# Convolution released ahead of the affine part, early transposes, residual products and a later last affine in a two-layer transformer kernel

## What is computed

```python
def short_conv_mixer(h, w_in, conv_w, conv_b, w_out):
    gb, gc, u = jnp.split(h @ w_in, 3, axis=-1)
    up = jnp.pad(gc * u, ((0, 0), (1, 1), (0, 0)))
    y = up[:, :-2] * conv_w[0] + up[:, 1:-1] * conv_w[1] + up[:, 2:] * conv_w[2] + conv_b
    return (gb * y) @ w_out

for l in range(DEPTH):
    ...
    u_lat = modulate(h_lat, m[0], m[1])
    ...
    h_lat = post_norm(h_lat, m[2] * y_lat, ln_w[l, 0], ln_b[l, 0])
    tokens = modulate(h_lat, m[3], m[4]).reshape(B * S, D)
    ...
    y = hier_moe(tokens, router_wg[l], router_bg[l], router_we[l], router_be[l], moe_w1[l], moe_w3[l], moe_w2[l])
    h_lat = post_norm(h_lat, m[5] * y[:B * S].reshape(B, S, D), ln_w[l, 1], ln_b[l, 1])
    ...
```

## Time and profile before

| | |
|---|---|
| median of three runs | 2521.5 us |
| the profiled execution: time, span | 2521.79 us, 2520.0 us |
| TensorE busy | 2326.1 us, 92% |
| VectorE, ScalarE, GpSimd busy | 30%, 17%, 11% |
| mean granted clock of TensorE | 0.962 |
| share of TensorE in the chain that ended last | 75% |
| share of DMA, VectorE in that chain | 10%, 7% |

### The profile page before, as it was taken

One profiled execution on the slowest core, in us unless ns is written; L12 is line 12 of the kernel. 1 busy time (PEld: TensorE's weight loads), 2 busy tenths in 40 slices (PEclk: granted clock), 3 DMA queues, 4 the chain that ended last, 5 costly groups with the idle time before them and its releaser, 6 DMA issues.

```text
span 2520.0 us, 28374 instructions
## 1 busy us (share of the span) xinstructions
PE 2326.1 (92%) x10444; PEld 1168.0 (46%) x10444; DVE 768.3 (30%) x1753; ACT 419.2 (17%) x912; POOL 280.7 (11%) x341
## 2 busy tenths in 40 slices
PE   6999999999995999999898699999995999999987
PEld 3556547887553344344343244444553343443332
DVE  2683115555545111111113411111344111111115
ACT  2301224443121101011013100000111101101111
POOL 0000104232223000000000000000232000000000
PEclk9999999999996999999999799999996999999998
DMA  9881000001127999999967010101009999999956
GB/s 386 303 330 45 1 0 2 2 18 55 58 75 305 420 421 412 417 395 421 421 278 263 19 50 25 50 25 67 25 34 378 420 421 409 413 406 421 421 222 250
DMA packets 137069, 572.28 MB, mean 227 GB/s; under 512 B 25033, under 2 KB 50793, under 8 KB 84458
## 3 DMA queue, kind: packets, MB, share of 16 engines
q1 hardware_dynamic: 123690, 536.97, 53.5%
q0 software_dynamic: 13248, 33.57, 3.4%
HBM read 549.51 MB, written 35.65 MB: 232 GB/s over the span
## 4 chain that ended last, share of the span: by engine, by line
PE 75%; DMA 10%; DVE 7%; SPq 2%; issue 2%; ACT 1%; POOL 1%; DVEq 0%; POOLq 0%; ACTq 0%
PE bank L1038 20%; PE bank L1110 13%; PE bank L1060 10%; PE bank L658 8%; DMA bigA<-in_moe_w 7%; PE bank L965 4%; PE bank L925 4%; PE bank L761 3%; PE bank L615 3%; DVE lnwb L1451 2%; SPq L428 2%; PE bank L775 1%; PE bank L1126 1%; PE bank L744 1%; POOL bigC L2026 1%
## 5 line engine op out<-in xcount | busy, mean ns | idle before, releaser
L1038 PE MATMUL bank<-bigA,bigB 128*32 128x512 f32 (+2 forms) x1968 | 472.4, 606 | 16.4 <-DMA bigA<-in_moe_w 11.9
L1110 PE MATMUL bank<-bigB,bigA 128*128 128x512 f32 x768 | 332.8, 596 | 20.8 <-DVEq L1949 20.8
L658 PE MATMUL bank<-bigC,bigB 128*128 128x512 f32 (+3 forms) x768 | 295.0, 540 | 0.0
L1060 PE MATMUL bank<-bigA,bigB 128*32 128x512 f32 (+2 forms) x1120 | 272.7, 607 | 14.7 <-DMA bigA<-in_moe_w 12.2
L1038 PEld LDWEIGHTS bank<-bigA,bigB 128*32 128x32 f32 (+2 forms) x1968 | 163.1, 137 | 258.1 <-issue 252.7
L1038 PE MATMUL bank<-bigC,bigB 128*128 128x512 f32 (+2 forms) x720 | 265.7, 599 | 9.2 <-DMA bigA<-in_moe_w 6.0
L1110 PEld LDWEIGHTS bank<-bigB,bigA 128*128 128x128 f32 x768 | 146.9, 191 | 206.3 <-issue 206.3
L658 PEld LDWEIGHTS bank<-bigC,bigB 128*128 128x128 f32 x768 | 144.3, 195 | 128.4 <-issue 119.5
L1171 ACT ACTIVATE bigB<-bank,small 128x128 f32<-128x128 f32 x288 | 107.6, 460 | 421.4 <-PE bank L615 421.4
L1060 PEld LDWEIGHTS bank<-bigA,bigB 128*32 128x32 f32 (+2 forms) x1120 | 98.9, 140 | 161.0 <-issue 156.7
L1038 PEld LDWEIGHTS bank<-bigC,bigB 128*128 128x128 f32 (+2 forms) x720 | 91.1, 151 | 134.0 <-issue 129.9
(11 more groups left out here) (278 smaller groups left out, 2298.9 us busy)
## 6 DMA issues: line engine op xcount, KB each, us to landing
bigA<-in_moe_w SPq DMA_DIRECT2D x292, 1024.0 KB, 21.5
bigC<-in_moe_w SPq DMA_DIRECT2D x92, 1024.0 KB, 23.2
bigA<-in_ada_w SPq DMA_DIRECT2D x40, 1024.0 KB, 7.2
bigA<-y_rows SPq DMA_DIRECT2D x16, 1024.0 KB, 4.9
bigA<-in_w_in_odd SPq DMA_DIRECT2D x24, 512.0 KB, 6.0
bigA<-in_ada_w SPq DMA_DIRECT2D x4, 2048.0 KB, 12.5
bigC<-in_w_in_even SPq DMA_DIRECT2D x4, 2048.0 KB, 14.3
h_rows<-bigC SPq DMA_DIRECT2D x16, 512.0 KB, 2.6
```

What stands on the lines that cost most here:

```text
L658: last = mm(bank(n % 3)[:, 0:w], uT[:, k, t * P:(t + 1) * P], wring[:, g % 2, k, at_:at_ + w], start=(k == 0), stop=(k == KC - 1))
L1038: last = mm(bank(m)[at_:at_ + w, :], xT[:, j, KC // 2 * h + k, at_:at_ + w], w13_at[SLOT_OF[m, h, q][0]][:, k, :], start=(h == 0 and k == ...
L1060: last = mm(bank(6 + n)[at_:at_ + w, :], gT[:, 2 * h + k, at_:at_ + w], w2_at[SLOT_OF[2, h, q][0]][:, k, n * 512:(n + 1) * 512], start=(h ...
L1110: last = mm(bank(3 * half + m), wc[:, j, m, k, :], u1T[:, k, half * 512:(half + 1) * 512], start=(k == 0), stop=(k == KC - 1))
```

## The change

- TensorE transposes the rows of steps 0 and 1 of the experts before it starts on step 0; step 1's go to banks 6 and 7 and are counted on `u_ev` and `u_ev_d`. Later steps keep their place. GpSimd's program is not changed; its gather for step 3 waits for the transposes of step 1, so it is released with them.
- Of tiles 0 and 1 at a layer's end, the products of alpha and the rows (`residual_part`) are issued right after the experts and wait for `hback` on a semaphore of its own; `combined` adds the experts' rows when `pair` is there. The sums use banks 4, 5 and 0, 1.
- In layer 0 the gate rows follow `combined(0, 0)` and `combined(0, 1)` on TensorE and ScalarE, in place of both ahead of them; banks of `stream_T` are changed to fit.
- VectorE clears the edges and raises `conv_d` before the eight affines of layer 0, not after them.
- In layer 1 the affine of tile t - 1 follows the statistics of tile t.

```diff
@@ -555,7 +555,7 @@
...
                 for t in range(2):
-                    load(hback[:, t], h_dram[l][t * P:(t + 1) * P, :], f"pair_in{t}")
+                    load(hback[:, t], h_dram[l][t * P:(t + 1) * P, :], f"x_in{t}")
                 with sp.Fori(0, OVER // 2) as i:
...
@@ -1017,16 +1017,20 @@
...
 
-                def gathered_T(b, j, loads):
+                def gathered_T(b, j, loads, at_=2):
 
                     pe.wait_ge(S(f"xg_in{l}_{j}"), 16 * loads)
-                    transposes(xg[:, j], 2).then_inc(S(f"x_T{l}"), 1)
+                    transposes(xg[:, j], at_).then_inc(S(f"x_T{l}"), 1)
 
...
                     if m == 0:
-                        pe.wait_ge(S(f"xT_ev{l}"), 2 * (b + 1))
+                        if b == 1:
+                            pe.wait_ge(S("u_ev"), 2 * NTC - 2 + l + 1)
+                            pe.wait_ge(S("u_ev_d"), 2 + l + 1)
+                        else:
+                            pe.wait_ge(S(f"xT_ev{l}"), max(2 * b, 2))
                         if b:
...
@@ -1062,14 +1066,16 @@
...
 
+
                 gathered_T(0, 0, 1)
+                gathered_T(1, 1, 1, 6)
                 for b in range(NB):
...
                     hidden_half(b, 1)
-                    gathered_T(b + 1, (b + 1) % 2, (b + 1) // 2 + 1)
                     if b:
+                        gathered_T(b + 1, (b + 1) % 2, (b + 1) // 2 + 1)
                         output(b - 1)
...
@@ -1077,7 +1083,7 @@
...
                     b = 2 * i + j
-                    pe.wait_ge(S(f"xT_ev{l}"), 2 * (b + 1))
+                    pe.wait_ge(S(f"xT_ev{l}"), 2 * b)
                     pe.wait_ge(S(f"silu_a{l}"), b)
...
@@ -1111,37 +1117,53 @@
...
 
+
+            def sum_at(t):
+                return (4, 0)[t % 2]
+
+            def residual_part(l, t):
+
+                if t < 2:
+                    pe.wait_ge(S(f"x_in{t}"), (128, 112)[t] + 16 * (l + 1))
+                else:
+                    pe.wait_ge(S(f"pair_in{t % 2}"), 112 * l + 16 + 32 * (t // 2))
+                    pe.wait_ge(S("nrm"), NT * (2 * l + 1) + t - 1)
+                for n in range(2):
+                    mm(bank(sum_at(t) + n), alpha_i[:, :], hback[:, t % 2, n * 512:(n + 1) * 512], start=True, stop=False,
+                       skip_group_check=True)
+
             def combined(l, t):
...
                     pe.wait_ge(S("share_ok"), l + 1)
-                pe.wait_ge(S(f"pair_in{t % 2}"), 32 * (NT // 2 * l + t // 2 + 1))
-                if t >= 2:
-                    pe.wait_ge(S("nrm"), NT * (2 * l + 1) + t - 1)
+                if t < 2:
+                    pe.wait_ge(S(f"pair_in{t}"), 112 * l + 16)
+                else:
+                    residual_part(l, t)
                 for n in range(2):
-                    cols_n = slice(n * 512, (n + 1) * 512)
-                    dst = bank(4 + 2 * (t % 2) + n)
-                    mm(dst, alpha_i[:, :], hback[:, t % 2, cols_n], start=True, stop=False)
                     for k in range(2):
-                        last = mm(dst, share[:, k, t, :], pair[:, t % 2, k, cols_n], start=False, stop=(k == 1))
+                        last = mm(bank(sum_at(t) + n), share[:, k, t, :], pair[:, t % 2, k, n * 512:(n + 1) * 512],
+                                  start=False, stop=(k == 1), skip_group_check=True)
                 last.then_inc(S("comb"), 1)
...
                 n = NT + t
-                if t == 0:
-                    pe.wait_ge(S("gate_ev"), 4)
-                if t >= 2:
+                if t < 2:
+                    pe.wait_ge(S("gate_ev"), t + 3)
+                else:
                     pe.wait_ge(S("tile_a"), n - 1)
                     pe.wait_ge(S("tile_d"), n - 1)
-                transposes(hh[:, t], 2 * (t % 2)).then_inc(S("tile_T"), 1)
+                transposes(hh[:, t], (2, 6)[t % 2]).then_inc(S("tile_T"), 1)
 
             moe(0)
-            gate_rows(2, diag1[:, 0], 0)
-            gate_rows(3, diag1[:, 1], 2)
+            for t in range(2):
+                residual_part(0, t)
             for t in range(NT):
                 combined(0, t)
+                if t < 2:
+                    gate_rows(t + 2, diag1[:, t], (2, 6)[t])
                 if t:
...
@@ -1155,6 +1177,8 @@
...
             moe(1)
+            for t in range(2):
+                residual_part(1, t)
             for t in range(NT):
...
@@ -1303,9 +1327,9 @@
...
 
-                def rows_T(b, j):
+                def rows_T(b, j, at_=2, done=f"xT_ev{l}"):
                     act.wait_ge(S(f"x_T{l}"), b + 1)
-                    modulated(xT[:, j], 2, mod_of(l, 1), f"xT_ev{l}")
+                    modulated(xT[:, j], at_, mod_of(l, 1), done)
 
...
@@ -1316,13 +1340,14 @@
...
                 rows_T(0, 0)
+                rows_T(1, 1, 6, "u_ev")
                 for b in range(NB):
...
                         gated(b - 1)
-                    rows_T(b + 1, (b + 1) % 2)
+                        rows_T(b + 1, (b + 1) % 2)
                 gated(NB - 1)
...
@@ -1358,17 +1383,17 @@
...
 
-                ln(2 * l + 1, t, banks[2 + t % 2][:, :])
+                ln(2 * l + 1, t, banks[(2, 0)[t % 2]][:, :])
 
...
                 act.wait_ge(S("tile_T"), NT + t + 1)
-                modulated(u1T[:, :, t * P:(t + 1) * P], 2 * (t % 2), normed_mod(1), "tile_a")
-
-            gate_row(2, 0, 0)
-            gate_row(3, 1, 2)
+                modulated(u1T[:, :, t * P:(t + 1) * P], (2, 6)[t % 2], normed_mod(1), "tile_a")
+
             for t in range(NT):
                 combined(0, t)
+                if t < 2:
+                    gate_row(t + 2, t, (2, 6)[t])
                 if t:
...
@@ -1869,12 +1894,13 @@
...
                 rows_T(0, 0)
+                rows_T(1, 1, 6, "u_ev_d")
                 for b in range(NB):
...
                     gate_up(b)
-                    rows_T(b + 1, (b + 1) % 2)
                     if b:
+                        rows_T(b + 1, (b + 1) % 2)
                         scattered(b - 1)
...
@@ -1899,7 +1925,7 @@
...
                 for n in range(2):
-                    half_stats(banks[2 + t % 2], n)
+                    half_stats(banks[(2, 0)[t % 2]], n)
                 ln_stats(2 * l + 1, t)
...
@@ -1932,15 +1958,13 @@
...
                 dve.wait_ge(S("tile_T"), NT + t + 1)
-                modulated(u1T[:, :, t * P:(t + 1) * P], 2 * (t % 2), normed_mod(1), "tile_d")
+                modulated(u1T[:, :, t * P:(t + 1) * P], (2, 6)[t % 2], normed_mod(1), "tile_d")
 
...
             stream_T(NT - 1)
-            for t in range(NT):
-                affine(0, t)
             dve.wait_ge(S("wa2_in"), 208)
...
@@ -1948,6 +1972,8 @@
...
             v.sem_inc(S("z_ok"), 2)
+            for t in range(NT):
+                affine(0, t)
             with dve.Fori(0, KC // 2) as i:
...
@@ -1979,7 +2005,9 @@
...
                 combined(1, t)
-                affine(1, t)
+                if t:
+                    affine(1, t - 1)
+            affine(1, NT - 1)
 
...
```

## The result

| | before | after |
|---|---|---|
| median (lowest to highest), four executions each | 2521.94 us (2520.18 to 2522.47) | 2497.56 us (2496.97 to 2498.24) |
| span of the profiled execution | 2520.0 us | 2495.2 us |
| mean granted clock of TensorE | 0.962 | 0.967 |
| TensorE, VectorE, ScalarE, GpSimd busy | 92%, 30%, 17%, 11% | 93%, 31%, 17%, 11% |

After over before is 0.9905, with a 95% interval of 0.9887 to 0.9922. The change takes off 24.4 us; the forecast was 2497.3 us. Of the executions on this page one, of `release_alone`, was slow (2554.08 us at a mean granted clock of 0.922) and is in no comparison.

A forecast was written before the change was run, and what follows sets the result against it. TensorE carries 75% of the chain, but full DMA engines set the expert stages' end. 19.1 + 1.8 + 2.8 + 0.5 + 0 = 24.2 us off 2521.8, less 0.3 to the median, gives 2497.3 us; range 2493.0 to 2500.8 with the near rivals.

The forecast's parts named there:

- A, the release: Layer 0's end: the convolution starts without waiting for VectorE's affines, which its first half covers; 19.1 us gained.
- B, layer 0's row products: Layer 0's end: residual products run while TensorE waits for the experts' rows; 1.8 us gained, between 1.0 and 2.3.
- C, layer 1's end: Residual products in the wait for experts' rows, affine a tile later; 2.8 us gained, bounds 0.9 and 3.2.
- VectorE's loop: Layer 1's end: 6.0 us a tile, just slower than loads and products at 5.73; the later affine makes it 4.8.
- this part's cost, the two affines at the end: Layer 1's end: two affines, 4.95 us, now come behind the last statistics and scale.
- One of my signs of being wrong: The prediction would be wrong if the residual products end after the experts' rows land.
- D, the clock: Convolution's first half: an earlier start saves 0.5 us of the 3.1 us that the low clock costs.
- The rival by which the convolution starts at 2.4 GHz: Convolution's start: clock comes back before the first product, all 3.1 us saved, 2494.7 us in total; chance 8%.
- E, the early transposes: Heads of both expert stages: step 1's products start 0.7 to 1.7 us earlier, the weights' wait takes it; 0 gained.
- The rival of the longer wait that costs clock: Expert stages: TensorE stands longer at the first weights' wait, clock stays low; 1.6 us a layer, 2500.5 us; chance 10%.
- The rival of the second gather: Expert stages: step 1's transposes hold step 0's products until a late second gather, slower than before; chance 2%.

The follow-up runs named there:

- release_alone: Kernel before with only the edge clears and the convolution's release put ahead of layer 0's eight affines: 2503.9 us, ratio 0.9933.
- after_again: The changed kernel itself, unedited, run again beside the later experiments: 2498.15 us, ratio 0.9907 to the kernel before.
- lag_alone: Kernel before with only layer 1's affine moved behind the next tile's statistics: 2521.03 us, ratio 1.0003.
- no_lag: Changed kernel with layer 1's affine back behind its own tile's statistics: 2498.32 us, ratio 0.9909 to the kernel before.
- warm_start: Changed kernel with idle TensorE products, three ahead of layer 0's last transposes and two behind: 2495.51 us, ratio 0.9902 to the kernel before.

## Why the prediction was right, point by point

**A, the release: 19.1 predicted, 18.9 measured** (18.4 alone, 18.2 in `after_again`). TensorE starts 0.46 us after ScalarE's last block (1392.31 + 2.91 = 1395.22, to 1395.68), where I took 0.2. The cover held as worked out: half 0 took 23.2 us, the affines 19.2.

**B, layer 0's row products: 1.8 predicted, 2.3 measured** (1.9 alone), at the upper bound, alone near the taken value. The residual products start at the low clock, 5.45 us for eight (0.50 is granted until about 1338.8); the nearest row, the gate rows' 5.68, was a fair price. TensorE still waits 1.2 us for the experts' rows behind them, 0.3 to 1.3 in the six executions that have them.

**C, layer 1's end: 2.8 predicted, 2.6 measured** (3.1 with the residual products alone). The size came, but one step of its reasoning failed: that "VectorE's loop of (2510.84 - 2468.92) / 7 = 6.0 us a tile was just slower than that 5.73", so that the later affine frees something. `lag_alone` shortened the loop and left the stretch at 41.96 us. Loads and products were as late as VectorE, not 0.27 us a tile ahead of it: with the affine out of the way the statistics wait for TensorE. I had also put this part's cost, the two affines at the end, inside the sum, and it is really there (1.05 us). Against it stands little: at the same clock the kernels with the later affine take 0.6 to 1.1 us longer from the first statistics to the end (the table under `no_lag` above), the loss that I had expected of it before `lag_alone` and `no_lag` ran. The whole gain of C comes from the residual products. It also varies more than this pair shows: `hback`'s issue to the end took 65.26 us here and 65.55 to 66.64 in the other four kernels built on the changed one, for 67.88 before. A step that the sum didn't have is the clock at tile 2: the wait for its load grew from 1.07 us to 2.58 to 2.83, and in three of six executions tile 2's products then ran at 0.50, for 1.4 us. One of my signs of being wrong came in part: in layer 1 the residual products end 0.1 us (here) to 1.1 us (`no_lag`) after the experts' rows land. The first statistics gained 3.3 us, not 3.7: tile 0's experts' rows start 12.90 us after `hback`'s issue where the kernel before began at 12.71, and from there to the statistics it takes 3.7 us where I had 3.4.

**D, the clock: 0.5 predicted, 0.7 in this pair of executions, and not shown to be a gain.** The first half took 22.70 to 23.95 us in the four executions without the release (before, and the three other parts alone) and 22.66 to 23.95 in the four with it and without a warm start. The row at 1397 was the right one to trust: the low level is granted before the long wait begins. The rival by which the convolution starts at 2.4 GHz didn't come, and `warm_start` shows its price, 2.3 us in the stretch (1.7 to 3.0 against all eight); I had priced the whole low clock at 3.1. The Trainium skill (TensorE: Matmul & The Clock Gate, Part 1: The HAM clock gate) says that the throttled level is the default and recent activity lifts it. `warm_start` agrees, once activity is put where it is missing. Applied to the removed wait alone the rule promised too much: one gap of 2.78 us and the transposes behind it were enough for 0.50.

**E, the early transposes: 0 predicted, -0.5 and -0.2 measured** (the same alone), no gain. The stage of layer 0 took 532.5 to 534.3 us in all executions with whole weights, so these are no loss either. One term was mis-sized: step 1's products start 2.8 us sooner after the gather (28.05 for 30.86), where I had 0.7 to 1.7. This pair is the extreme one: over all executions with whole weights it is 28.05 to 28.89 with the early transposes and 30.49 to 30.86 without, 2.0 us on the mean. TensorE by time at the head of the stage after, which answers to the earlier trace rows:

```profile
802.97 1.97 PE L615 MATMUL bank<-cst,bigB 128*128 128x128 f32 x8 [9.69 <-DMA bigB<-h_rows,ints]
806.23 1.97 PE L615 MATMUL bank<-cst,bigB 128*128 128x128 f32 x8 [1.29 <-DMA bigB<-h_rows,ints]
808.14 14.74 PE L1042 MATMUL bank<-bigA,bigB 128*64 128x512 f32 x64
822.71 7.03 PE L1042 MATMUL bank<-bigC,bigB 128*64 128x512 f32 x32
```

Step 0's products start 1.6 us later after the first transposes (5.17 for 3.57), priced at 2.0. But they take 14.74 us for 16.50: less of them lies at the low clock, and the whole delay comes back, not half of it. No stage became shorter, so the weights took it all, as said. TensorE's waits from 795 to 1303, before and after (the same lines of each list, total, times, longest):

```profile
PE bank L1038 <- DMA bigA<-in_moe_w: 9.9, 4, 3.7
...
PE bank L1060 <- DMA bigA<-in_moe_w: 5.9, 4, 3.8
...
PE bank L1038 <- DMA bigC<-in_moe_w: 0.2, 1, 0.2
```

```profile
PE bank L1042 <- DMA bigA<-in_moe_w: 10.7, 4, 3.6
PE bank L1064 <- DMA bigA<-in_moe_w: 7.4, 4, 3.8
PE bank L1042 <- DMA bigC<-in_moe_w: 0.4, 1, 0.4
```

That is 18.5 us for 16.0, 2.5 more beside the 2.8 won. Over the other executions these waits are 17.0 to 18.7 us with the early transposes and 16.4 to 17.4 without; the means are 1.5 us apart, beside the 2.0 won. The rival of the longer wait that costs clock had 1.6 us a layer; no stage grew by more than 0.5 between before and after, and layer 0's stages of the same code differ by more. The rival of the second gather needed a landing 16.5 us later; it landed 1.29 us after TensorE was free for it.

**The sum.** 18.92 + 2.31 + 2.62 + 0.73 - 0.65 = 23.93 us. With 0.83 from the two stretches of unchanged code that makes the 24.76 between the ends of the two profiled executions; the medians differ by 24.4. Predicted were 24.2. That the total came within 0.3 us is luck in part: unchanged code moves the start of the experts by up to 2 us either way, and C, with 2.6 us in this pair, was 1.2 to 2.3 in the other kernels built on the changed one.

## What to carry to other kernels

Before an engine's step is moved forward in a stage, look for waits of that stage that come later and belong to a stream at full rate: here the 2 us won at its head (mean of six executions) went into longer waits and left the stage as long as before, and 4 us a layer stayed only once the stream ran at half its rate. A semaphore raised behind work that its consumer doesn't need is the cheapest thing to find, by a long wait whose releaser is a queue and not data, and it is worth the wait less the next releaser. Where two limits are equally late, relieving one gives nothing: check what the relieved engine would wait for next before adding its price to a sum. Here the relief even cost 0.6 to 1.1 us, which no median showed and equal stretches at an equal clock did.

## What was not expected of the hardware

- A few idle products around short transposes held TensorE's clock at 1.00: ten instructions of 128x512 in gaps of 2.78 and 2.00 us brought a first half of 20.95 us in both kernels that have them, for 22.66 to 23.95 in all others with whole weights, without delaying its start.
- Wide products after a stand started at the low clock even where they are meant to fill a wait: eight residual products took 5.39 to 6.42 us, not 3.4. They are free only while their wait is longer than that.
- At one place either level was granted: after a wait of 2.6 to 2.8 us for tile 2's load in layer 1, three executions had 1.00 and three 0.50, and four products took 1.98 us or 3.38 to 3.41. Kernels with and without the later affine are on both sides, so that edit alone doesn't decide it; what does is open. It is 1.4 us that a comparison of two executions can put down to the wrong edit.
- Code that no kernel changed, up to the first gather, took between 792.7 and 796.5 us from one execution to another. A difference between two single executions of less than 4 us says nothing until it is cut into stretches.
